# Bias lines as sixteen shifted copies, wide up products in a row, first block and last tile split, TensorE spins

## The chip, the cores and the metric

The kernel runs on one core of a Trainium2 chip. A core has five engines with queues of their own: TensorE (matrix products, PE in the profile, its weight loads PEld), VectorE (DVE), ScalarE (ACT), GpSimd (POOL) and SyncE (SP), which here does nothing but issue DMAs. They meet through semaphores alone. The metric is device time in microseconds of one execution; the median of three runs is given.

## The reference, cut to what matters

Two transformer blocks, in float32, one after the other on the same 256 tokens of 1024 columns. The parts that the change touches:

```python
def first_block(x, ...):                       # layer 0: gated linear attention; layer 1: window attention
    h = x
    h = h + gla_mixer(rmsnorm(h, ln_mix[0]), a_w_in[0], ...)        # a_w_in: 1024 x 3088
    h = h + sq_relu_mlp(rmsnorm(h, ln_mlp[0]), w_up[0], w_down[0])  # up 1024 x 4096, down 4096 x 1024
    kb, vb = shared_kv(rmsnorm(h, kv_norm), w_kv)
    h = h + swa_mixer(rmsnorm(h, ln_mix[1]), kb, vb, ..., rel_table, ...)
    h = h + sq_relu_mlp(rmsnorm(h, ln_mlp[1]), w_up[1], w_down[1])
    return rmsnorm(h, ln_final)

  # swa_mixer:  s = q k^T + rel_table[bucket(i + 128 - j)]     a bias that depends on i - j alone
  # mixer_b:    sc = q k^T + rel_bias[t5_bucket(j - i)]        the same, three dilations, 12 heads

def second_block(x, p, ...):
    x = x + (gate_a * y_a + gate_b * y_b) @ w_out
    x = x + square(relu(rmsnorm_2(x, norm_mlp_g) @ w_ff1)) @ w_ff2
    gate_p = sigmoid(rmsnorm_2(x, norm_ple_g) @ w_ple_gate)         # 1024 x 1024
    x = x + gate_p * (p @ w_ple)
    return rmsnorm_2(x, final_norm_g)
```

## The kernel before, in words

**Products.** Every float32 matrix is held as a high part (rounded, float32r) and a low part (the rest). A product is three float32r products in one PSUM bank: high by high, high by low, low by high (`prod`). Activations are transposed to [column, token], eight groups of 128 columns, high and low (`hT`). 161 weight blocks of up to 128 x 2048 elements pass through three raw buffers and three high and low buffers. For each block SP issues one load (`weights_to`), ScalarE casts it to `whi` (`highs_to`, line 1695), VectorE subtracts to get `wlo` (`lows_to`, line 941, two halves), TensorE multiplies (line 265). SP issues the load of block j when the lows of block j - 3 are done. All loads and stores go through SP's one queue, in program order.

**Order.** Each engine has its own program (`tensor_program`, `vector_program`, `scalar_program`, `pool_program`, `sync_program`), written out by hand with generators (`gemm_a`, `gemm_up`, `gemm_b`) that step through the same blocks on each engine; nothing is reordered at run time. A wait holds its engine's whole queue.

**Start.** SP loads the identity, a gain, x in two halves of 512 columns, then weight block 0. TensorE transposes x in four pairs of 128 columns (`norm_turn`, line 269); ScalarE and VectorE write the high and low part of each pair times the gain; ScalarE casts block 0 and VectorE subtracts; then `gemm_a` multiplies it (two output halves of eight groups). Blocks 0 to 4 are queries, keys and a 16-column gate; 5 to 8 the values; 9 to 12 the output gate.

**Bias.** TensorE makes one line of bias per head with a selection matrix (16 lines of 383, 12 of 511). SP writes the lines to DRAM (`scr1`, `scr2`), then builds in DRAM the full 128-row shifted tables (`toe1` 16 x 128 x 256, `toe2` 12 x 128 x 384) with two DRAM-to-DRAM transfers, between the loads of blocks 6 and 7. Each table is loaded later by one transfer: after block 20, and after block 61.

**Up products.** Three times (both layers and the second block's MLP) `gemm_up` multiplies 1024 x 4096 in 16 blocks, interleaved with the 16 blocks of the down product. Weights stand still, tokens move: for each group of 128 rows one product of 512 columns (the high weights by [high | low] activations, `hT2`, two pieces of 256 columns 2048 elements apart) and one of 256 columns (low weights by high activations), which adds to the second half of the bank. In the first block the eight groups are done in two halves of four, with the transposes of the second half between.

**End.** `gemm_b` multiplies the last gate (`pg`) in four blocks, tokens in two halves c, columns in two halves f. For each of the four tiles: ScalarE's sigmoid, VectorE's product with `pw` and sum into x, ScalarE's square with a sum, GpSimd's mean and power, VectorE's final multiply by row scale and gain, SP's store.

## Time and profile before

| | us |
|---|---|
| median of three runs | 1066.18 (1065.83 to 1066.78) |
| the profiled execution | 1064.24 |
| span of its instructions | 1062.4 |
| TensorE busy | 1012.1 (95%) |
| VectorE, ScalarE, GpSimd busy | 676.2, 489.3, 42.8 |
| chain that ended last: TensorE | 85% |
| 180.99 MB moved by DMA, mean | 170 GB/s |

All profile numbers come from one execution, the one of 1064.24 us; times in its views count from the start of its span. A row of the timeline gives start, duration, engine, line of the code, operation, what is written from what, shape and count; the bracket tells how long the engine was idle before and what ended that. Consecutive instructions of one kind are merged in a row. A product's duration reaches to its modelled end, past the start of the next, so the spacing is read from starts. A chain row gives what TensorE or another engine did, or waited for, on the way to the last instruction.

### The profile page before, as it was taken

What the parts mean: (1) busy time and instruction counts of PE and PEld (TensorE: products, weight loads), DVE (VectorE), ACT (ScalarE), POOL (GpSimd) and SP (SyncE); (2) the same over time, 40 slices, a digit from 0 to 9 for tenths busy, and PEclk for the clock granted to TensorE, in tenths of its full rate; (3) what the DMA queues carried; (4) which work ended last, traced back from release to release, by engine and by line L of the source; (5) the groups of instructions that cost most, each with busy time, mean ns of one, the idle gap of its engine ahead of it and who ended that gap; (6) DMA issues with size and microseconds to landing.
All of it is one profiled execution on the core that took longest, in us unless ns stands there. A gap on an engine that the chain in (4) does not pass through costs nothing.

```text
span 1062.4 us, 12980 instructions
## 1 busy us (share of the span) xinstructions
PE 1012.1 (95%) x5384; PEld 849.5 (80%) x5384; DVE 676.2 (64%) x945; ACT 489.3 (46%) x573; POOL 42.8 (4%) x57
## 2 busy tenths in 40 slices
PE   6989999999999889999999999899999999999996
PEld 5866778888888767888888889877877788888875
DVE  4665766566656885754666656676656675466664
ACT  4353445344445653544444454334563454344452
POOL 1000100000000000000000013300000000000000
PEclk9989999999999999999999999999999999999999
DMA  7772376545564314765455555632335656545451
GB/s 214 249 262 80 119 238 224 173 160 197 199 214 143 120 50 149 250 217 197 159 188 180 201 183 161 196 100 80 99 109 178 195 175 215 188 159 197 180 175 43
DMA packets 115027, 180.99 MB, mean 170 GB/s; under 512 B 4351, under 2 KB 78567, under 8 KB 114968
## 3 DMA queue, kind: packets, MB, share of 16 engines
q1 hardware_dynamic: 114968, 180.16, 50.8%
q8 instruction: 42, 0.69, 0.3%
q14 instruction: 17, 0.14, 0.0%
HBM read 179.05 MB, written 5.55 MB: 174 GB/s over the span
## 4 chain that ended last, share of the span: by engine, by line
PE 85%; DVE 7%; ACT 2%; DMA 2%; POOL 2%; issue 1%; SPq 0%; DVEq 0%; POOLq 0%; ACTq 0%
PE ps L265 82%; PE ps L269 3%; DMA raw<-in_a_w_in 2%; DVE wlo L941 2%; DVE M L949 1%; DVE M L941 1%; POOL st L2186 1%; ACT M L1692 1%; ACT RR L1695 1%; ACT whi L1695 1%; POOL M L2186 0%; DVE M L945 0%; ACT M L1695 0%; DMA x<-in_x 0%; POOL st L2183 0%
## 5 line engine op out<-in xcount | busy, mean ns | idle before, releaser
L265 PE MATMUL ps<-whi,RR 128*128 128x512 f32 (+2 forms) x1568 | 494.6, 390 | 9.7 <-DVE wlo L941 6.0
L1695 ACT ACTIVATE whi<-raw 128x2048 fp32r<-128x2048 f32 (+1 forms) x161 | 302.3, 1881 | 196.6 <-PE ps L265 179.9
L941 DVE TENSOR_TENSOR wlo<-raw,whi 128x1024 fp32r<-128x1024 f32 (+1 forms) x322 | 372.5, 1200 | 29.9 <-ACT whi L1695 29.7
L265 PE MATMUL ps<-RR,whi 128*128 128x512 f32 (+1 forms) x1248 | 362.8, 357 | 10.9 <-DVE RR L949 5.6
L265 PEld LDWEIGHTS ps<-whi,RR 128*128 128x128 f32 x1568 | 293.9, 189 | 74.8 <-issue 9.6
L265 PE MATMUL ps<-wlo,RR 128*128 128x512 f32 (+2 forms) x784 | 303.2, 387 | 0.0
L265 PE MATMUL ps<-RR,wlo 128*128 128x256 f32 (+1 forms) x1008 | 284.5, 282 | 0.0
L265 PEld LDWEIGHTS ps<-RR,whi 128*128 128x128 f32 x1248 | 220.3, 190 | 50.6 <-issue 8.3
L265 PEld LDWEIGHTS ps<-RR,wlo 128*128 128x128 f32 (+1 forms) x1008 | 191.5, 190 | 0.9
L265 PEld LDWEIGHTS ps<-wlo,RR 128*128 128x128 f32 x784 | 148.4, 189 | 27.7
L941 DVE TENSOR_TENSOR M<-M,ps 128x512 f32<-128x512 f32 x56 | 38.5, 687 | 181.7 <-ACT M L1695 173.8
L1695 ACT ACTIVATE M<-ps 128x512 f32<-128x512 f32 (+2 forms) x97 | 57.1, 597 | 173.7 <-PE ps L265 138.5
L265 PE MATMUL ps<-M 128*64 128x128 f32 (+5 forms) x416 | 66.4, 334 | 5.6 <-DVE M L949 2.9
L265 PEld LDWEIGHTS ps<-M 128*64 128x64 f32 (+2 forms) x416 | 46.6, 163 | 22.1 <-issue 13.2
L1695 ACT ACTIVATE RR<-M 128x512 fp32r<-128x512 f32 x48 | 30.4, 633 | 71.1 <-DVE M L949 71.1
L2183 POOL TENSOR_SCALAR st<-st 128x2 f32<-128x2 f32 (+3 forms) x13 | 7.7, 595 | 886.6 <-DVE st L1032 621.3
L269 PE MATMUL ps<-ident,M 128*128 128x128 f32 (+1 forms) x194 | 29.4, 290 | 13.3 <-DVE M L941 4.9
L1695 ACT ACTIVATE RR<-ps,G 128x256 fp32r<-128x256 f32 x64 | 25.1, 480 | 32.9 <-PE ps L269 32.8
L269 PEld LDWEIGHTS ps<-ident,M 128*128 128x128 f32 (+1 forms) x194 | 23.2, 148 | 20.9 <-issue 14.9
L949 DVE SCALAR_TENSOR_TENSOR M<-M 128x512 f32<-128x512 f32 (+1 forms) x49 | 34.4, 703 | 1.6
L949 DVE SCALAR_TENSOR_TENSOR RR<-ps,G,RR 128x256 fp32r<-128x256 f32 x64 | 26.4, 478 | 13.7 <-ACT RR L1695 13.7
L941 DVE TENSOR_TENSOR RR<-M,RR 128x512 fp32r<-128x512 f32 x48 | 32.9, 686 | 0.0
(88 smaller groups left out, 381.7 us busy)
## 6 DMA issues: line engine op xcount, KB each, us to landing
raw<-in_w_up SPq DMA_DIRECT2D x32, 1024.0 KB, 5.4
raw<-in_w_down SPq DMA_DIRECT2D x32, 1024.0 KB, 5.0
raw<-in_w_ff SPq DMA_DIRECT2D x32, 1024.0 KB, 5.3
raw<-in_w_in SPq DMA_DIRECT2D x23, 1024.0 KB, 5.1
raw<-in_a_w_in SPq DMA_DIRECT2D x12, 1024.0 KB, 7.1
raw<-in_a_w_out SPq DMA_DIRECT2D x4, 1024.0 KB, 5.0
raw<-in_b_w_q SPq DMA_DIRECT2D x4, 1024.0 KB, 5.3
raw<-in_b_w_out SPq DMA_DIRECT2D x4, 1024.0 KB, 5.0
```

The lines of the kernel that those rows point to most:

```text
L265: return pe.matmul(out, lhsT, rhs, start=start, stop=stop, skip_group_check=True)
L269: return pe.transpose(out, in_, ident[0:n, 0:n])
L941: return dve.tensor_tensor(out, a, b, op)
L949: return dve.scalar_tensor_tensor(out=out, in0=a, scalar=s, in1=b, op0=op0, op1=op1)
L1692: return act.activation(out, in_, f, **k)
L1695: return act.activation(out, in_, ACT.Copy, **k)
L2183: return pool.tensor_scalar(out, a, s1, s2, op0, op1)
L2186: return pool.tensor_tensor(out, a, b, op)
```

## The change

Four edits.

1. The first weight block is loaded in two halves, each behind one half of x; ScalarE and VectorE treat it in halves between the pairs of transposed columns; TensorE does its first four groups of both output halves before the other four, and the row-scale product one block later. TensorE begins with four products of a matrix of ones by itself, written to a bank that nothing reads, and does five more behind the transpose of the gain. GpSimd writes the ones first.
2. Each bias line is written to DRAM sixteen times, each copy one element further on; the two tables are gone. Each of eight transfers per table fills sixteen rows straight from the copies, one ahead of each of eight weight blocks.
3. `hT` holds high and low of a group next to each other, so that `hT2` is one piece; `gemm_up` does the wide products of a row of groups first, behind the wait for the highs, then the narrow ones behind the wait for the lows.
4. The last quarter of the last gate is done as two tiles of 256 columns. The final gain is multiplied into a second buffer before the row scale is known; ScalarE does the final scale of the first token half, VectorE that of the second; GpSimd adds the sums step by step.

```diff
-        self.hT, self.yT = parts(0), parts(4096)
-        self.hT2 = RR[:, 0:4096].rearrange("p (a k t) -> p k a t", a=2, t=T)
+        self.hT2 = RR[:, 0:4096].rearrange("p (k n) -> p k n", k=8)
+        self.hT, self.yT = (self.hT2[:, :, 0:T], self.hT2[:, :, T:2 * T]), parts(4096)
...
+LAST = [(0, 0, 512), (1, 0, 512), (0, 512, 1024), (1, 512, 768), (1, 768, 1024)]
...
-            for w_ in due(K.at("w_lo", j)):
-                pe.wait_ge(*w_)
...
-                        for w_ in due(ready(k)):
+                        for w_ in due(K.at("w_lo", (0, 0) if j == 0 and k < 4 else j), ready(k)):
                             pe.wait_ge(*w_)
...
-            for w_ in due(K.at("w_lo", j)):
+            for w_ in due(K.at("w_hi", j)):
                 pe.wait_ge(*w_)
...
                     for k in range(k0, k1):
                         for w_ in due(ready(k)):
                             pe.wait_ge(*w_)
-                        mm(b[:, i, :].rearrange("p (a t) -> p a t", a=2), hi[:, k, 128 * i:128 * i + 128],
-                           V.hT2[:, k, :, :], k == 0, False)
+                        mm(b[:, i, :], hi[:, k, 128 * i:128 * i + 128], V.hT2[:, k, :], k == 0, False)
+                    for w_ in due(K.at("w_lo", j)):
+                        pe.wait_ge(*w_)
+                    for k in range(k0, k1):
                         t = mm(b[:, i, T:2 * T], lo[:, k, 128 * i:128 * i + 128], hT[0][:, k, :], False, k == 7)
...
+    def spin(n):
+        for w in due(K.at("ones")):
+            pe.wait_ge(*w)
+        for _ in range(n):
+            mm(K.banks[:, 3, 0:128], V.S["ones"][:, :], V.S["ones"][:, :], True, True)
+    spin(4)
     tile = ("g", 0)
     b = take(tile, misc())
     for w in due(K.dma("id"), K.dma("g0")):
         pe.wait_ge(*w)
     tr(b[:, 0:16], V.M[0:16, 0:128]).then_inc(*K.filled(tile))
+    spin(5)
     norm_rest(0)
...
     def after_qk(f):
-        if f == 0:
+        if f == 256:
             rows_scale(0)
...
-    g = gemm_a(("qk",), W, 0, 1024, hT, h_ready(0), None, after_qk)
+    g = gemm_a(("qk",), W, 0, 1024, hT, h_ready(0), lambda: None, after_qk)
...
-    run_all((gemm_b(("pg",), A["w_ple_gate_2"][0], 0, D, hT, h_ready(6)), 1))
+    ready = h_ready(6)
+    for f in (0, 512):
+        bs = acc_pair()
+        tiles = [(("pg", i), take(("pg", i), misc() if i == 4 else bs[LAST[i][0]])) + LAST[i]
+                 for i in range(5) if LAST[i][1] // 512 * 512 == f]
+        for k0 in (0, 4):
+            j, hi, lo = block(A["w_ple_gate_2"][0][k0 * 128:k0 * 128 + 512, f:f + 512], 4, 512)
+            for tile, b, c, n0, n1 in tiles:
+                for k in range(k0, k0 + 4):
+                    for w in due(K.at("w_lo", j), ready(k)):
+                        pe.wait_ge(*w)
+                    t = prod(b[:, 0:n1 - n0], hT[0][:, k, c * 128:c * 128 + 128], hT[1][:, k, c * 128:c * 128 + 128],
+                             hi[:, k - k0, n0 - f:n1 - f], lo[:, k - k0, n0 - f:n1 - f], k == 0, k == 7)
+                if k0:
+                    t.then_inc(*K.filled(tile))
...
+    def first_low(i):
+        h = slice(1024 * i, 1024 * i + 1024)
+        for w in due(K.at("w_hi", (0, 0) if i == 0 else 0)):
+            dve.wait_ge(*w)
+        tt(V.lo[:, 0, h], V.raw[:, 0, h], V.hi[:, 0, h].bitcast(F32), ALU.subtract).then_inc(
+            *K.up("w_lo", (0, 0) if i == 0 else 0))
+    norm_early(0)
+    first_low(0)
+    norm_turn(0, 2)
+    norm_turn(0, 3)
+    first_low(1)
+    block["lo"] = 1
...
     def ev_qk(f):
-        tile = ("qk", f)
         if f == 0:
             diagonals(0)
+        if f == 256:
             rows_scale(0)
...
+        for f2 in {0: [], 256: [0, 256]}.get(f, [f]):
+            tile = ("qk", f2)
+            for w in due(K.full(tile), *rb(0)):
+                dve.wait_ge(*w)
+            stt(M[:, 2 * f2:2 * f2 + 512], K.bank(tile), 128 ** -0.5 if f2 < 512 else 1.0, RB[:, :], ALU.mult,
+                ALU.mult).then_inc(*K.emptied(tile))
...
-    run_all((gemm_b(1024, 8, ev_pg), 1))
...
+    def add(i):
+        c, n0, n1 = LAST[i]
+        s, xc, n = V.SG[:, c, n0:n1], x[:, c, n0:n1], n0 // 512
+        for w in due(K.empty(("pg", i)), K.empty(("pw", 512 * n, c))):
+            dve.wait_ge(*w)
+        d = step(tt(s, s, V.PW[:, c, n0:n1], ALU.mult))
+        for w in due(d, K.full(("nt", 6, 3)), x_ready(K, 6, c, n)):
+            dve.wait_ge(*w)
+        tt(xc, xc, s, ALU.add).then_inc(*K.up("x_end", i))
...
+    def gain(i):
+        c, n0, n1 = LAST[i]
+        for w in due(K.at("x_end", i), K.dma("fin")):
+            dve.wait_ge(*w)
+        tt(V.SG[:, c, n0:n1], x[:, c, n0:n1], M[:, n0:n1], ALU.mult).then_inc(*K.up("x_gain", i))
...
+    take()
+    take()
+    add(0)
+    add(1)
+    take()
+    gain(0)
+    gain(1)
+    take()
+    for i in (2, 3, 4):
+        add(i)
+    for i in (2, 3, 4):
+        gain(i)
+    for n in range(2):
+        s = V.SG[:, 1, 512 * n:512 * n + 512]
+        for w in due(K.at("rstd", ("end", 1)), K.at("x_gain", 4)):
+            dve.wait_ge(*w)
+        ts(s, s, st[:, 49:50], None, ALU.mult, None).then_inc(*K.up("y_end", (1, n)))
...
+    def first_high(i):
+        h = slice(1024 * i, 1024 * i + 1024)
+        for w in due(K.dma("w_first") if i == 0 else K.dma("w0", 0)):
+            act.wait_ge(*w)
+        copy(V.hi[:, 0, h], V.raw[:, 0, h]).then_inc(*K.up("w_hi", (0, 0) if i == 0 else 0))
+    norm_early(0)
+    first_high(0)
+    norm_turn(0, 2)
+    norm_turn(0, 3)
+    first_high(1)
+    block["hi"] = 1
...
+    def square(i):
+        c, n0, n1 = LAST[i]
+        for w in due(K.at("x_end", i)):
+            act.wait_ge(*w)
+        actf(V.PW[:, c, n0:n1], x[:, c, n0:n1], ACT.Square, scale=1.0 / 32, accum_out=st[:, 40 + i:41 + i]).then_inc(
+            *K.up("end_sq", i))
+    take()
+    take()
+    for i in range(2):
+        sig(i)
+        square(i)
+    take()
+    take()
+    sig(2)
+    sig(3)
+    square(2)
+    sig(4)
+    square(3)
+    square(4)
+    for n in range(2):
+        s = V.SG[:, 0, 512 * n:512 * n + 512]
+        for w in due(K.at("rstd", ("end", 0)), K.at("x_gain", 2)):
+            act.wait_ge(*w)
+        copy(s, s, scale=st[:, 48:49]).then_inc(*K.up("y_first", (0, n)))
...
+        ts(st[:, 52 + c:53 + c], st[:, 40 + c:41 + c], EPS, None, ALU.add, None).then_inc(*K.up("end_sum", c))
+    at = [52, 53]
+    for c, i in ((0, 2), (1, 3), (1, 4)):
+        for w in due(K.at("end_sum", at[c] - 52), K.at("end_sq", i)):
             pool.wait_ge(*w)
-        ts(st[:, 46 + c:47 + c], st[:, 44 + c:45 + c], 1.0 / D, EPS, ALU.mult, ALU.add).then_inc(
...
+        tt(st[:, 52 + i:53 + i], st[:, at[c]:at[c] + 1], st[:, 40 + i:41 + i], ALU.add).then_inc(*K.up("end_sum", i))
+        at[c] = 52 + i
+        if i != 3:
+            for w in due(K.at("end_sum", i)):
+                pool.wait_ge(*w)
+            tt(st[:, 48 + c:49 + c], st[:, at[c]:at[c] + 1], S["half_"][:, 0:1], ALU.pow).then_inc(
+                *K.up("rstd", ("end", c)))
...
     for n in range(2):
         load("x%d" % n, 0, V.x[:, :, n * 512:n * 512 + 512], xd[:, :, n * 512:n * 512 + 512])
+        w = K.blocks[0][0][512 * n:512 * n + 512, :] if K.blocks else A["a_w_in"][0][0:512, 0:256]
+        load("w0" if n else "w_first", 0, V.raw[:, 0, 1024 * n:1024 * n + 1024].rearrange("p (k n) -> p k n", k=4),
+             w.rearrange("(k p) n -> p k n", p=128))
+    state["block"] = 1
...
-    load("scr1", 0, A["scr1"], M[0:16, 14336:14719], K.empty(("br", 0)))
+    line = M[0:16, 14336:14719]
+    load("scr1", 0, bass.AP(tensor=A["scr1"].tensor, offset=0, ap=[[400, 16], [16 * 400 + 1, 16], [1, 383]]),
+         bass.AP(tensor=line.tensor, offset=line.offset, ap=[line.ap[0], [0, 16], [1, 383]]), K.empty(("br", 0)))
     for g in range(3):
-        load("scr2", g, A["scr2"][4 * g:4 * g + 4, :], M[32 * g:32 * g + 4, 14848:15359], K.empty(("br", g + 1)))
-    load("toe1", 0, A["toe1"], bass.AP(tensor=A["scr1"].tensor, offset=127, ap=[[383, 16], [-1, 128], [1, 256]]),
-         K.dma("scr1"))
-    load("toe2", 0, A["toe2"], bass.AP(tensor=A["scr2"].tensor, offset=127, ap=[[511, 12], [-1, 128], [1, 384]]),
-         K.dma("scr2", 2))
+        line = M[32 * g:32 * g + 4, 14848:15359]
+        load("scr2", g, bass.AP(tensor=A["scr2"].tensor, offset=4 * g * 528,
+                                ap=[[528, 4], [12 * 528 + 1, 16], [1, 511]]),
+             bass.AP(tensor=line.tensor, offset=line.offset, ap=[line.ap[0], [0, 16], [1, 511]]),
+             K.empty(("br", g + 1)))
...
-    weights_to(21)
-    load("bias", 0, V.BS, A["toe1"].rearrange("h p c -> p h c"), K.dma("toe1"), K.full(("to", 1, 1)))
-    weights_to(62)
-    load("bias", 1, V.BB, A["toe2"].rearrange("h p c -> p h c"), K.dma("toe2"), K.empty(("pr", 1, 1)))
+    for a in range(8):
+        weights_to(20 + a)
+        load("bias1", a, V.BS[16 * a:16 * a + 16], bass.AP(tensor=A["scr1"].tensor, offset=127 - 16 * a, ap=[
+            [16 * 400, 16], [400, 16], [1, 256]]), K.dma("scr1"), K.full(("to", 1, 1)))
+    weights_to(60)
+    for a in range(8):
+        weights_to(61 + a)
+        load("bias2", a, V.BB[16 * a:16 * a + 16], bass.AP(tensor=A["scr2"].tensor, offset=127 - 16 * a, ap=[
+            [12 * 528, 16], [528, 12], [1, 384]]), K.dma("scr2", 2), K.empty(("pr", 1, 1)))
...
             load("out", 2 * c + n, A["out"][0, c * 128:c * 128 + 128, n * 512:n * 512 + 512],
-                 V.x[:, c, n * 512:n * 512 + 512], K.at("y_end", (c, n)))
+                 V.SG[:, c, n * 512:n * 512 + 512], K.at("y_end" if c else "y_first", (c, n)))
...
-        A["scr1"] = nc.dram_tensor("scr1", (16, 383), F32, kind="Internal").ap()
-        A["scr2"] = nc.dram_tensor("scr2", (12, 511), F32, kind="Internal").ap()
-        A["toe1"] = nc.dram_tensor("toe1", (16, 128, 256), F32, kind="Internal").ap()
-        A["toe2"] = nc.dram_tensor("toe2", (12, 128, 384), F32, kind="Internal").ap()
+        A["scr1"] = nc.dram_tensor("scr1", (16, 16, 400), F32, kind="Internal").ap()
+        A["scr2"] = nc.dram_tensor("scr2", (16, 12, 528), F32, kind="Internal").ap()
```

Where the change moves instructions, the order on two engines follows. Line numbers of the changed kernel are its own. In the rows, `ps` is a PSUM bank, `RR` the activations, `whi` and `wlo` the weights' parts, moving operand first.

TensorE, the program's beginning, before:

```order
L269 MATMUL ps<-ident,M 128x16 [waits d_g0,d_id]
L269 MATMUL ps<-ident,x 128x128 [waits d_x0]
L269 MATMUL ps<-ident,x 128x128 x7
L269 MATMUL ps<-ident,x 128x128 [waits d_x1]
L269 MATMUL ps<-ident,x 128x128 x3
L269 MATMUL ps<-ident,x 128x128 [waits ps4_read]
L269 MATMUL ps<-ident,x 128x128 x3
L265 MATMUL ps<-RR,whi 128x256 [waits w_lo,ps5_read]
```

and now:

```order
L267 MATMUL ps<-ones 128x128 [waits ones]
L267 MATMUL ps<-ones 128x128 x3
L271 MATMUL ps<-ident,M 128x16 [waits d_g0,d_id]
L267 MATMUL ps<-ones 128x128 x5
L271 MATMUL ps<-ident,x 128x128 [waits d_x0]
L271 MATMUL ps<-ident,x 128x128 x7
L271 MATMUL ps<-ident,x 128x128 [waits d_x1]
L271 MATMUL ps<-ident,x 128x128 x3
L271 MATMUL ps<-ident,x 128x128 [waits ps4_read]
L271 MATMUL ps<-ident,x 128x128 x3
L267 MATMUL ps<-RR,whi 128x256 [waits w_lo,ps5_read]
```

The spins stand ahead of the gain's transpose and of x's; further down, the wait for the block's second half stands before the 25th product.

TensorE, the first block of the first up product, before (the rest of the half goes on in the same way):

```order
L265 MATMUL ps<-RR,whi 128x512 [waits ps4_read,w_lo]
L265 MATMUL ps<-RR,wlo 128x256
L265 MATMUL ps<-RR,whi 128x512
L265 MATMUL ps<-RR,wlo 128x256
L265 MATMUL ps<-RR,whi 128x512 [waits ps5_read]
L265 MATMUL ps<-RR,wlo 128x256
```

and now, with the beginning of the second half:

```order
L267 MATMUL ps<-RR,whi 128x512 [waits ps4_read,w_hi]
L267 MATMUL ps<-RR,whi 128x512
L267 MATMUL ps<-RR,whi 128x512 [waits ps5_read]
L267 MATMUL ps<-RR,whi 128x512
L267 MATMUL ps<-RR,wlo 128x256 [waits w_lo]
L267 MATMUL ps<-RR,wlo 128x256 x3
L267 MATMUL ps<-RR,whi 128x512 x4
L267 MATMUL ps<-RR,wlo 128x256 x4
L271 MATMUL ps<-ident,x 128x128 [waits ps2_read]
L271 MATMUL ps<-ident,x 128x128 [waits ps3_read]
L271 MATMUL ps<-ident,x 128x128 x6
L267 MATMUL ps<-RR,whi 128x512 [waits ps4_read]
```

Four wide products stand in a row, then four narrow ones, where they alternated.

SP, from the bias lines on (`scr` the lines in DRAM, `toe` the tables, `raw` weight blocks), before:

```order
L2293 DMA scr<-M 16x383 [waits ps6_read]
L2293 DMA scr<-M 4x511 [waits ps7_read]
L2293 DMA scr<-M 4x511 [waits ps4_read]
L2293 DMA scr<-M 4x511 [waits ps5_read]
L2293 DMA toe<-scr 2048x1x256 [waits d_scr1]
L2293 DMA toe<-scr 1536x1x384 [waits d_scr2]
L2303 DMA raw<-in_a_w_in 128x4x512 [waits w_lo] x2
```

and now:

```order
L2389 DMA scr<-M 16x16x383 [waits ps6_read]
L2389 DMA scr<-M 4x16x511 [waits ps7_read]
L2389 DMA scr<-M 4x16x511 [waits ps4_read]
L2389 DMA scr<-M 4x16x511 [waits ps5_read]
L2399 DMA raw<-in_a_w_in 128x4x512 [waits w_lo] x2
```

The two transfers to `toe` are gone from between the lines and the loads of blocks 7 and 8. Sixteen-row pieces (`M<-scr 16x16x256`) stand further down, one ahead of the fourth block of the first up product and of each of the seven behind it, where one load of a table stood behind the fourth.

## Rows read from the trace of the kernel before

**Rows 1.** The page, busy time, share of the span and count by engine.
```profile
PE 1012.1 (95%) x5384; PEld 849.5 (80%) x5384; DVE 676.2 (64%) x945; ACT 489.3 (46%) x573; POOL 42.8 (4%) x57
```

**Rows 2.** TensorE's busy time (count), granted clock, DMA share, GB/s in seven stretches.
```profile
14.38:20.21 5.83, 5.83 (x27) 1.00 0.73 205
23.44:28.83 5.39, 5.39 (x47) 1.00 0.90 297
61.23:65.66 4.43, 0.20 (x1) 0.88 0.72 265
65.67:71.41 5.74, 5.74 (x14) 0.50 0.58 194
152.30:324.80 172.50, 172.50 (x870) 1.00 0.57 193
869.81:878.66 8.85, 8.85 (x41) 1.00 0.73 262
879.11:883.69 4.58, 4.58 (x27) 1.00 0.87 305
```

**Rows 3.** Timeline of the start: start, us, engine, line, operation, count.
```profile
5.50 3.67 PE L269 MATMUL ps<-ident,x 128*128 128x128 f32 x16 [2.17 <-DMA x<-in_x]
6.65 3.40 ACT L1695 ACTIVATE RR<-ps,G 128x256 fp32r<-128x256 f32 x8 [1.74 <-PE ps L269]
7.61 3.35 DVE L949 SCALAR_TENSOR_TENSOR RR<-ps,G,RR 128x256 fp32r<-128x256 f32 x8 [4.06 <-ACT RR L1695]
9.94 1.91 ACT L1695 ACTIVATE whi<-raw 128x2048 fp32r<-128x2048 f32 x1
...
11.88 2.36 DVE L941 TENSOR_TENSOR wlo<-raw,whi 128x1024 fp32r<-128x1024 f32 x2 [0.92 <-ACT whi L1695]
...
15.30 2.35 DVE L941 TENSOR_TENSOR wlo<-raw,whi 128x1024 fp32r<-128x1024 f32 x2
```

**Rows 4.** DMA issues, us to landing, stretches 2.2:2.5 and 2.7:3.0.
```profile
x<-in_x SPq DMA_DIRECT2D x1, 512.0 KB, 4.7
...
raw<-in_a_w_in SPq DMA_DIRECT2D x1, 1024.0 KB, 7.2
```

**Rows 5.** Chain that ended last, 30 to 75 us: start, us, what.
```profile
40.08 21.20 DMA raw<-in_a_w_in
...
65.67 8.42 PE ps L265 x24
```

**Rows 6.** Timeline of VectorE and of ScalarE, 28 to 110 us.
```profile
58.02 1.22 DVE L941 TENSOR_TENSOR M<-M 128x1024 f32<-128x1024 f32 x1
...
64.53 2.95 ACT L1692 ACTIVATE M<-M 128x1024 f32<-128x1024 f32 x3
```

**Rows 7.** DMA issues of the whole run: count, KB, us to landing.
```profile
M<-toe SPq DMA_DIRECT2D x1, 2048.0 KB, 12.4
...
scr<-M SPq DMA_DIRECT2D x1, 23.9 KB, 4.3
```

**Rows 8.** Timeline of VectorE and of TensorE, 149.5 to 153.8 us.
```profile
151.30 1.66 DVE L949 SCALAR_TENSOR_TENSOR RR<-ps,G,RR 128x256 fp32r<-128x256 f32 x4 [1.16 <-ACT RR L1695]
...
152.23 0.50 PE L265 MATMUL ps<-RR,whi 128*128 128x512 f32 x1 [1.40 <-DVE RR L949]
```

**Rows 9.** Timeline of the end.
```profile
1053.38 0.39 PE L265 MATMUL ps<-whi,RR 128*128 128x512 f32 x1
...
1053.89 0.67 ACT L1692 ACTIVATE M<-ps,st 128x512 f32<-128x512 f32 x1
...
1058.34 1.41 DVE L949 SCALAR_TENSOR_TENSOR x<-x,st,M 128x512 f32<-128x512 f32 x2 [1.00 <-POOL st L2186]
...
1059.12 0.99 SPq L2293 DMA_DIRECT2D out<-x  x2
```

**Rows 10.** Groups by shape: count, busy us, mean ns, idle before.
```profile
L1692 ACT ACTIVATE M<-ps,cc 128x256 f32<-128x256 f32 x16 | 7.4, 470 | 16.2 <-DVE cc L945 16.2
...
L941 DVE TENSOR_TENSOR RR<-ps,RR 128x256 fp32r<-128x256 f32 x18 | 7.6, 422 | 6.1 <-ACT RR L1695 5.8
```

58 lines of the change are left out of this document (14 added, 44 removed).

## The prediction

> **What bounds the kernel now.** I read the page first: TensorE is busy 95% of the span [rows 1], so a microsecond counts only where TensorE waits, where its products are spaced wider than they need be, or behind its last product. The view of busy time by stretch comes next, since it counts products and names the granted clock [rows 2]. In all four places that the change touches, TensorE loses something: it starts its first weight product at 14.38 and runs 27 of them in 5.83 us (216 ns each, against 120 ns later for the same shape: the 1.2 GHz level by the spacing, although the column still reads 1.00); it stands still before 65.67 and then works at a granted clock of 0.50; in the up products a pair takes more than its two halves do elsewhere; and 9.0 us pass between the start of the last product and the end. The timeline of the start, the chain of waits, and the tail give the steps [rows 3, 5, 9].
>
> **First block split, and spins.** Today the first product waits for all eight transposed columns and the whole weight block: ScalarE writes eight gains (0.43 us each from 6.65) and casts the block in 1.91, VectorE subtracts for 2.36, end 14.24 [rows 3]. The loads keep one queue: the second half of x lands 4.7 us after its issue at about 2.1, thus at 6.8, and the first 1 MB block at about 2.6 + 7.2 = 9.8, 3.0 us for a megabyte [rows 4]. Afterwards half a block (1.5 us) stands ahead of the second half of x, so x is complete at 8.3 and the block, as before, at 9.8. ScalarE: four gains to 8.35, half a cast to 9.4, four gains to 11.1, half a cast to 12.2. VectorE is one step behind: half the lows at 10.65, four gains to 12.35, the other half to 13.6. TensorE stands in order behind the transposes of the late half of x (8.3 to 10.0), which are done before 10.65, so they cost nothing. It starts at 10.8; 24 products at 120 ns end at 13.7, 24 more at 16.6. Block 1 then waits: ScalarE squares x (1.1) behind its cast at 12.2, casts block 1 (1.9), VectorE subtracts (2.35): 17.65, the very time of today [rows 3], because this chain does not get shorter. Block 1 begins at 17.8 instead of 22.73 (20.21 + 21 x 0.120). The row-scale product only changes its place. A later evacuation (the low products' 16-row tile, now behind two evacuations and a low) takes back some 0.25 us on a PSUM bank. Gain 4.9 - 0.3 = **4.6 us**. It rests on the clock: nine spins and sixteen transposes fill most of 1.0 to 10 us, and the rows show the level rising twice after some 5.8 us of unbroken work (14.38 to 20.21, 65.67 to 71.41 [rows 2]); the 3.67 us of transposes alone did not raise it [rows 3]. If it stays low, the first 24 products take 5.2 us and the sum is 3.4 us: the lower end. The later half of the small loads leaves SP only 0.6 us earlier; the blocks that it feeds are wanted several microseconds after they land, so nothing is lost there.
>
> **Bias lines.** Two DRAM-to-DRAM writes of 2.0 and 2.25 MB leave the queue; behind them block 7 took 21.2 us to land [rows 5], and TensorE, whose last product of block 6 starts just before 61.23, has 0.20 us of work until block 7 begins at 65.67 [rows 2]. They are replaced by four writes of 0.78 MB together. At the rate of the 2 MB load (12.4 us [rows 7]) that is 4.7 us; if each of the four took the 4.3 us of today's 24 KB write [rows 7], 17 us, and block 7 would land near 58. (It cannot go by bytes from that row, as 1 MB lands in 7.2 us at worst in [rows 4].) I take 4.7, since rows of 1 to 2 KB are moved in both; either way the load itself costs at most 0.7 us. What is late next is VectorE: its subtraction for the gates ends at 58.02 + 1.22 = 59.24 [rows 6], the lows of block 7 follow, 2.36, so TensorE starts at 61.65. Twenty-four products at 227 ns end at 67.1. Next in TensorE's order are transposes of the decayed keys: VectorE multiplies queries and keys (twice 1.2, as at 58.02; ScalarE's three exponentials take 2.95 [rows 6] and no longer queue behind the block-7 cast), subtracts block 8 (2.36) and multiplies the decayed keys (1.22), 67.5. Today block 7 ended near 74.0 because its products ran at a granted 0.50 until 71.41 [rows 2, 5]. So 74.0 - 67.6 = **6.4 us**, with 4.4 (only the standstill goes) and 7.0 (no wait at 67.1) as ends.
> The rest of the part moves loads: two of 2.0 and 2.25 MB become sixteen of 256 to 288 KB, one ahead of each weight block of the two first up-and-down products. By today's load a piece takes 12.4 / 8 = 1.55 us. A weight block has 172.5 us / 30.5 = 5.65 us, and the engines are busy 0.57 of it [rows 2], which leaves 2.4 us: hidden. The first piece of the second set waits for the last evacuation of the attention output with one more weight block now behind it; that block is the fourth to be used, three block times of 5.65 us later. Cost 0.
>
> **Up product.** All 768 pairs of a 512-column and a 256-column product are reordered, wide ones in a row, and the wide operand becomes one piece of memory instead of two. In the mixed stream 26 products start in 4.58 us, 352 ns a pair. A stream of 512-column products alone has 39 starts in 8.85 us, 226.9 ns; one of 256-column products 45 starts in 5.39, 119.8 [rows 2] (one or two products run into each stretch and are in its count). Together 346.7, 5.6 ns less: 768 x 5.6 = 4.3 us. Against it: in the first chunk of each of the three up products TensorE resumes behind VectorE's four lows of 1.66 us [rows 8]. Today it does wide, narrow, wide, narrow there while the second pair of lows is made; in a row, the third wide one is reached after 0.55 us and waits some 0.3 us, 0.8 us in three chunks. Net **3.5 us**, ends 4.3 gained and 0.8 lost. The wait on the highs instead of the lows frees nothing, since lows are long done in these stages.
> A rule speaks against this term. The Trainium skill, "TensorE: Matmul & The Clock Gate", section "Back-to-back issue gap", gives the spacing of products as columns over 2.4 GHz plus 2.5 ns, so that a pair takes the same time in any order. The unmixed streams here carry 13 ns each over their columns, not 2.5; whether the 5.6 ns on top belong to the order no run here shows.
>
> **Last tile split.** Today, from the start of the last product (1053.38): sigmoid 1053.89, two VectorE steps, square, three GpSimd steps, two final multiplies from 1058.34 to 1059.75, that is 6.37 us, then issue and landing to 1062.4 [rows 9]. Afterwards the last tile has 256 columns: product to sigmoid 0.40, sigmoid 0.47, two VectorE steps of 0.42 [rows 10], square and its sum 0.5, add and power 0.9 to 1.2, two multiplies by a scalar 0.9, hops 0.2: 4.2 to 4.5. The gain multiplies fit in between the square and the power. That is 2.0 less; the two halves cost 48 x 0.120 - 24 x 0.227 = 0.31 more on TensorE. Net **1.5 us**, ends 0.9 and 2.0.
>
> **Sum.** 4.6 + 6.4 + 3.5 + 1.5 = 16.0. The profiled run took 1064.24 us, 1.94 below the median of 1066.18: 1064.24 - 16.0 = 1048.2, on the median 1050.2. The stages between are bound by TensorE and move forward whole.
>
> **Rivals.** (1) Spacing is set by columns alone: the 352 ns remain, only the new 0.8 us wait is left, 16.0 - 4.3 = 11.7 gained, 1054.5. For it: VectorE and ScalarE cannot cause it, and both widths carry an equal fixed part. Against it: a pair is longer than its parts, and both things that differ are removed. The section cited above would have it so. 0.18. (2) The spins do not do what they are for and the level rises only during the first block: 14.8 gained, 1051.4. For it: the transposes did not raise it. 0.17. (3) Slower: a bias piece, written to 16 rows, moves at a fraction of today's rate and holds up the weight block behind it in the same queue, sixteen times. Beyond 2.4 us a piece the queue falls behind, with some 6 us in hand per product (loads run two blocks ahead); at 5 us a piece 2 x (8 x 2.6 - 6) = 29.6 lost, 1079.8; it outweighs the gains from 4.2 us a piece. Against it: 1.55 us by [rows 7]. 0.05. The Trainium skill, "SBUF — State Buffer", section "Door 1", has 16 partitions reach 4 of 16 ports, 104 GB/s against 328 for 128; an estimate from it is 2.5 us a piece, just at the room of 2.4, which would still leave the sum as it is; no run here shows it.
>
> **How the numbers follow.** Forecast 1050.2, chance 0.57, its own range 1047.9 (all upper ends) to 1053; (1) 0.18, (2) 0.17, (3) 0.05, the rest for cases between. Range 1046.5 to 1056.5, which takes in (1) and (2), and (1) with (2) at 1055.7. A measurement can tell about 0.2% (2.1 us): faster 0.93, same 0.02, slower 0.05.
>
> **What would show it.** Right: first weight product near 10.8 at 120 ns; no granted 0.50 around 65; block 7 landing in 10 us or less; 347 ns a pair; the last issue about 5 us behind the last product's start. Wrong: casts of weights that wait for DMA in the first two up products; 216 ns in the first block; 352 ns a pair with a wait of 0.3 us in each first chunk.

## The result, and the profile after

The changed kernel takes 1054.26 us (median of four runs, 1053.28 to 1056.38), the kernel before, on the same chip, 1066.01. The ratio is 0.9898, with an interval of 0.9872 to 0.9925: 11.8 us less where 16.0 were forecast. The time lies inside the range, 4.1 us above the forecast and above the forecast's own range of 1047.9 to 1053. That it lies 0.2 us from rival (1)'s 1054.5 is chance: the mechanism of that rival is refuted below (experiments 3 and 4). The profiled execution took 1055.0 us, its span is 1053.2.

The page of the changed kernel, busy time by engine (the answer to [rows 1]):

```profile
PE 1014.0 (96%) x5426; PEld 853.6 (81%) x5426; DVE 677.0 (64%) x950; ACT 491.5 (47%) x579; POOL 42.7 (4%) x58
```

The page counts 42 product records more on TensorE (each of the nine spins is two records, and the split last quarter adds 24), and the span is 9.2 us shorter. Where those come from is read from the starts of the same instructions in both traces. Each number says by how many microseconds the instruction starts earlier than in the kernel before:

| TensorE's place (start before) | forecast | changed | changed, again | no spins | copies in DRAM |
|---|---|---|---|---|---|
| block 1 (23.02; the forecast counts from 22.73) | 4.9 | 5.4 | 5.1 | 5.2 | 5.2 |
| transposes of the decayed keys (73.92) | 11.0 | 9.2 | 9.0 | 8.7 | 11.0 |
| first up product, second half (152.23) | 11.0 | 7.7 | 9.0 | 8.7 | 9.5 |
| second up product (424.35) | 12.2 | 7.1 | 9.7 | 8.4 | 8.7 |
| third up product (848.58) | 13.3 | 7.9 | 10.4 | 8.8 | 9.4 |
| last product (1053.38) | 14.2 | 8.0 | 10.5 | 8.9 | 9.5 |
| end of the span (1062.4) | 16.0 | 9.2 | 11.8 | 10.2 | 10.8 |

("Changed, again" is the same kernel, profiled a second time; the last two columns are experiments below. In the first row 0.3 us of each measured number are the row-scale products, which only change their place: counted from 22.73 it is 5.1, 4.8, 4.9 and 4.9.) The first block gains what was forecast. Then 1.8 us are missing at the decayed keys; the up products add less than 1.2 us each; the tail adds 1.2 to 1.3 where 1.8 were expected; and in the attention stages of the first trace 2.8 us are lost that the second keeps (1.5 between the decayed keys and the first up product, 1.3 before the second).

The start on VectorE and TensorE, timeline of the changed kernel (start, duration, what):

```profile
9.14 1.23 DVE L970 TENSOR_TENSOR wlo<-raw,whi 128x1024 fp32r<-128x1024 f32 x1
...
15.18 2.36 DVE L970 TENSOR_TENSOR wlo<-raw,whi 128x1024 fp32r<-128x1024 f32 x2 [0.76 <-ACT whi L1755]
```

```profile
8.80 1.09 PE L271 MATMUL ps<-ident,x 128*128 128x128 f32 x8 [1.77 <-DMA x<-in_x]
10.51 0.77 PE L267 MATMUL ps<-RR,whi 128*128 128x256 f32 x2 [0.62 <-DVE wlo L970]
...
17.59 0.50 PE L267 MATMUL ps<-RR,whi 128*128 128x256 f32 x2
```

The lows of the block's first half are done at 10.37 and the product starts at 10.51; block 1 starts at 17.59 behind its lows (15.18 + 2.36). Forecast were 10.65, 10.8 and 17.8. One of the prediction's signs of being wrong appears all the same: the first dozen products start 213 ns apart, at a granted 0.50 from 9.92 to 13.34, and TensorE's own 48 products end only at 17.59, together with those lows.

The same kernel's chain that ended last, 28 to 66 us, against [rows 5]:

```profile
32.52 3.71 SPq L2389
...
36.28 16.72 DMA raw<-in_a_w_in
...
64.70 0.63 PE ps L271 x4
```

The 21.20 us of block 7's load are now 16.72, not under 10. SP itself is held (3.71 us to issue one of the copies). But this row is not yet the key to the 1.8 us. VectorE in the same trace (the multiplication for the gates, the lows of block 7, those of block 8):

```profile
54.90 1.23 DVE L970 TENSOR_TENSOR M<-M 128x1024 f32<-128x1024 f32 x1
56.05 2.35 DVE L970 TENSOR_TENSOR wlo<-raw,whi 128x1024 fp32r<-128x1024 f32 x2
...
61.05 2.36 DVE L970 TENSOR_TENSOR wlo<-raw,whi 128x1024 fp32r<-128x1024 f32 x2 [0.20 <-ACT whi L1755]
```

The lows of block 7 do not wait. VectorE comes to the multiplication at 54.90, where it comes at 53.59 without spins and at 53.61 with the copies in DRAM, in two traces that have no stretch at 0.50 around 30. Between 31 and 37 us TensorE's place falls from 0.3 to 1.3 us behind the trace without spins. So some 1.3 of the 1.8 us go to the stretch from 30.40 to 33.82 (below), and some 0.5 to waits behind block 7; in the second trace (54.90 becomes 55.15) it is 1.5 of 2.0. Where that stretch is missing, the late landing alone costs 2.3 us (experiment 6).

TensorE's granted clock in stretches of the changed kernel (busy time and counts by engine, then granted clock, DMA share, GB/s), and below it, when the same kernel was profiled again, its own stretch at 31.52 and the stages that stood at 85.02 and 351.26:

```profile
9.92:13.34 3.42, 2.83 (x13) 2.86 (x14) 3.40 (x7) 3.24 (x8) 0.00 (x0) 0.50 0.88 237
30.40:33.82 3.42, 3.42 (x14) 2.94 (x14) 3.30 (x4) 2.69 (x2) 0.00 (x0) 0.50 1.03 364
85.02:88.43 3.41, 3.41 (x8) 1.08 (x6) 0.00 (x0) 0.00 (x0) 0.00 (x0) 0.50 0.00 0
351.26:354.67 3.41, 2.88 (x14) 2.92 (x15) 3.27 (x11) 1.85 (x7) 0.20 (x1) 0.50 0.29 117
```

```profile
31.52:34.94 3.42, 3.42 (x19) 3.42 (x18) 2.72 (x3) 1.91 (x1) 0.00 (x0) 0.50 0.99 326
85.22:88.63 3.41, 3.41 (x14) 1.81 (x13) 0.59 (x3) 1.26 (x2) 0.00 (x0) 1.00 0.02 5
350.00:353.40 3.40, 2.88 (x25) 2.91 (x26) 3.26 (x11) 1.85 (x7) 0.20 (x1) 1.00 0.32 131
```

The stretch at 0.50 around 65 [rows 2] is gone, as forecast; others came. Of the four shown, two (85.0 and 351.3) are missing in the second trace of the same kernel; the other two come again, 1.1 us later. Its stage at 350 does 25 products where the first did 14, and its stage at 85 does fourteen where the first did eight.

### The profile page after: what moved, and what is told of

It reads as the page before. It is cut to its first block, busy times and chain, and to the rows that moved or that the text cites. A ratio compares the mean times of both kernels' runs of the same rounds, so it can differ in the third digit from the quotient of the medians.

```text
span 1053.2 us, 13094 instructions
## 1 busy us (share of the span) xinstructions
PE 1014.0 (96%) x5426; PEld 853.6 (81%) x5426; DVE 677.0 (64%) x950; ACT 491.5 (47%) x579; POOL 42.7 (4%) x58
## 3 DMA queue, kind: packets, MB, share of 16 engines
HBM read 174.60 MB, written 1.83 MB: 168 GB/s over the span
## 4 chain that ended last, share of the span: by engine, by line
PE 82%; DVE 8%; ACT 3%; DMA 2%; POOL 2%; issue 1%; SPq 0%; POOLq 0%; DVEq 0%; ACTq 0%
PE ps L267 79%; PE ps L271 3%; DVE wlo L970 2%; DMA raw<-in_a_w_in 2%; DVE M L978 1%; DVE M L970 1%; ACT M L1752 1%; POOL st L2279 1%; ACT whi L1755 1%; DVE M L974 1%; DVE RR L978 1%; SPq L2389 0%; ACT RR L1755 0%; POOL M L2279 0%; ACT M L1755 0%
## 5 line engine op out<-in xcount | busy, mean ns | idle before, releaser
L1755 ACT ACTIVATE whi<-raw 128x2048 fp32r<-128x2048 f32 (+2 forms) x162 | 302.6, 1871 | 192.6 <-PE ps L267 155.5
L267 PE MATMUL ps<-RR,whi 128*128 128x512 f32 (+1 forms) x1248 | 285.9, 354 | 6.5 <-DVE RR L978 5.6
L267 PEld LDWEIGHTS ps<-RR,whi 128*128 128x128 f32 x1248 | 215.2, 191 | 37.8 <-DVE RR L978 8.5
L267 PE MATMUL ps<-RR,wlo 128*128 128x256 f32 (+1 forms) x1008 | 177.1, 284 | 0.0
L267 PEld LDWEIGHTS ps<-RR,wlo 128*128 128x128 f32 (+1 forms) x1008 | 152.2, 191 | 8.2
L1755 ACT ACTIVATE RR<-M 128x512 fp32r<-128x512 f32 x48 | 30.4, 633 | 71.1 <-DVE M L978 71.1
L2276 POOL TENSOR_SCALAR st<-st 128x2 f32<-128x2 f32 (+2 forms) x11 | 6.5, 594 | 882.8 <-DVE st L1061 618.8
```

The source lines that it names most:

```text
L267: return pe.matmul(out, lhsT, rhs, start=start, stop=stop, skip_group_check=True)
L1755: return act.activation(out, in_, ACT.Copy, **k)
L2276: return pool.tensor_scalar(out, a, s1, s2, op0, op1)
```

## Experiments

The kernels ran in three groups (1 to 4, 5 to 8, 9 to 12), each on one chip beside the kernel before, whose medians there are 1063.13, 1064.03 and 1065.17.

**1. No spins.**

```diff
-    spin(4)
-    spin(5)
```

> The changed kernel without its nine products of ones at the start. Theory (clock): in the changed kernel the spins brought the 2.4 GHz level at 6.5 us, but a stretch at a granted 0.50 from 9.92 to 13.34 took it back, so only some 13 of the first 24 weight products were spared. Without spins the level rises during the first block: the first 24 products at 213 to 216 ns, block 1 starting 0 to 1.2 us later than the 17.59 of the changed kernel, and the whole 0 to 1.5 us slower than it (1053 to 1056). Rival (the spins carry most of the start's gain): block 1 starts at 19 or later and the whole is over 2 us slower. Second question: if the 0.50 stretches at 30.4 and 85.0 follow from the early lift, they are gone here, and the whole is 1 to 3 us faster.

Measured: 1053.64 (1053.21 to 1055.25), ratio 0.991, 0.9895 to 0.9925: the changed kernel's time. TensorE, timeline without spins:

```profile
17.78 0.50 PE L267 MATMUL ps<-RR,whi 128*128 128x256 f32 x2 [0.76 <-DVE wlo L968]
```

The spacing falls from 213 to some 118 ns at 11.7 by itself; block 1 starts 0.2 us later than with spins, after a wait for VectorE's lows. The spins are worth nothing that the times show. But that VectorE sets block 1 is not general: over all traces 1 to 17 of the first 24 products are slow with the spins and 5 to 19 without them, and with many slow ones TensorE comes last. In the second trace of the changed kernel 17 are slow, and block 1 starts at 17.95, 0.65 us behind its lows. In this trace the stretches at 30 and 85 are at 1.00, but experiments 5 and 6 below, also without spins, have one of them or both again.

**2. More spins,** which fill TensorE's standstills at 7.0 and 9.9.

```diff
-    norm_rest(0)
+    norm_early(0)
+    spin(6)
+    norm_turn(0, 2)
+    norm_turn(0, 3)
+    spin(2)
```

> The changed kernel with six more products of ones between the two halves of the transposes (7.03 to 8.80, where TensorE stands still for 1.77 us) and two before the first weight product. Theory (the 0.50 stretch at 9.92 follows that standstill): no granted 0.50 before 13.3, the first 24 products at 120 ns (10.5 to 13.4). Block 1 still starts at 17.5 because VectorE's second lows set it, so this by itself gives at most 0.3 us; if the stretch at 30.4 goes with it, another 1.5 to 2.0 us. Rival (the stretches come whatever TensorE did just before): 0.50 again near 9.9 and 30.4, 213 ns in the first half, time as the changed kernel within 0.5 us.

Measured: 1054.5 (1053.81 to 1055.14). Stretches of this kernel:

```profile
10.30:13.20 2.90, 2.90 (x25) 2.90 (x24) 2.76 (x5) 2.81 (x6) 0.00 (x0) 1.00 0.89 224
29.90:36.70 6.80, 6.80 (x27) 5.13 (x25) 4.10 (x5) 2.12 (x2) 0.00 (x0) 0.50 0.76 222
```

The first half of the block runs at 2.4 GHz, as the theory had it, and TensorE then waits 1.16 us for the lows of block 1. The stretch at 30 did not go along; it is longer. So that half of the expectation fell. Nor is the filled standstill shown to be the reason: two kernels of other experiments with the changed kernel's own start (3 and 8) had no 0.50 before 29 either.

**3. and 4. The order alone, and the layout alone.** First the wide operand in two pieces again, order kept (`hT` as before, and the wide product reads the two pieces):

```diff
-        self.hT2 = RR[:, 0:4096].rearrange("p (k n) -> p k n", k=8)
+        self.hT2 = RR[:, 0:4096].rearrange("p (a k t) -> p k a t", a=2, t=T)
...
```

> The changed kernel with the old layout of the activations, so that the wide operand is two pieces of 256 columns again; only the order (wide products in a row) is kept. Theory (the order makes the spacing): 64 products of the up product take 11.15 us as in the changed kernel (348 ns a pair). Rival (the two pieces make it): 11.29 us, 353 ns a pair.

Then one piece, with wide and narrow products alternating (the wait for the lows comes first again):

```diff
...
                         mm(b[:, i, :], hi[:, k, 128 * i:128 * i + 128], V.hT2[:, k, :], k == 0, False)
-                    for w_ in due(K.at("w_lo", j)):
-                        pe.wait_ge(*w_)
-                    for k in range(k0, k1):
                         t = mm(b[:, i, T:2 * T], lo[:, k, 128 * i:128 * i + 128], hT[0][:, k, :], False, k == 7)
```

> The changed kernel with wide and narrow products alternating as before; only the layout in one piece is kept. Theory (the order makes the spacing): 64 products take 11.29 us as before the change (353 ns a pair), the first chunks lose their new waits (second half of the first chunk back to the old pace), so the whole is 2 to 2.5 us slower than the changed kernel. Rival (the layout makes it): 11.15 us, and the whole is 1 to 2 us faster than the changed kernel.

Measured: 64 products of the third up product, from their first start to the start of the next product, in the changed kernel, order alone, layout alone, and in the kernel before (one to two products of the neighbours are in the counts):

```profile
871.64:882.78 11.14, 11.14 (x65) 9.82 (x64) 4.25 (x5) 4.96 (x4) 0.00 (x0) 1.00 0.35 122
```

```profile
871.14:882.28 11.14, 11.14 (x65) 9.82 (x64) 4.25 (x5) 4.96 (x4) 0.00 (x0) 1.00 0.35 126
```

```profile
872.09:883.38 11.29, 11.29 (x66) 9.82 (x64) 4.25 (x5) 4.96 (x4) 0.00 (x0) 1.00 0.35 124
```

```profile
879.11:890.40 11.29, 11.29 (x65) 9.79 (x64) 4.25 (x5) 4.96 (x4) 0.00 (x0) 1.00 0.36 124
```

The order does it, the layout nothing: 348.3 ns a pair against 352.8. In starts, the order alone gains 1.0, 0.7 and 0.7 us in the three up products, as the changed kernel does; the layout alone gains 0.3, then loses 0.5 and 0.3. Times: 1056.12 and 1056.68, two runs each, too few to order them. One part of the expectation was wrong: with the layout alone the first chunk of the second and third up product takes 19.97 us, as in the changed kernel, where 19.61 (before) was expected. There the alternating stream itself was slower, at 353 ns a pair, than in the kernel before, at 347 (last section).

**5. Copies not shifted against each other** (without spins; `scr1` in the same way). The kernel leaves out the shift, so the bias that it adds is another.

```diff
-                                ap=[[528, 4], [12 * 528 + 1, 16], [1, 511]]),
+                                ap=[[528, 4], [12 * 528, 16], [1, 511]]),
```

> Without spins, and with the sixteen copies of a bias line not shifted against each other (the same bytes and rows, but every copy starts on the same boundary; the bias that is added is therefore another). In the changed kernel without spins block 7 lands at 53.55, 16 us behind its issue, and in 36 to 50 us the queue moves only 23 to 50 GB/s. Theory (a copy is read from four rows of the on-chip memory, and four rows give little): nothing changes, block 7 lands at 52 to 54. Rival (writes that start 4 bytes apart are slow): block 7 lands before 45, and the transposes of the decayed keys start near 63.2 instead of 65.25.

Measured: block 7 lands at 53.79, 17.67 us behind its issue; 1056.11 us. Alignment is not it. What the queue moves from 28 to 57 us in the changed kernel, in forty slices (busy share of 16 DMA engines in tenths, GB/s):

```profile
DMA  9999999993223222258999478997425632277999
GB/s 379 387 322 305 347 401 398 363 206 57 23 23 48 25 28 23 25 59 147 271 330 328 102 138 229 319 328 243 116 71 170 211 122 102 106 129 207 380 408 379
```

From 34.5 to 40 us two to three tenths of the engines are busy, at 23 to 57 GB/s. The three copies of 128 KB that come from four rows are moving, and block 7 waits behind them. The other one, 383 KB from sixteen rows, landed 6.0 us after its issue. The Trainium skill, "DMA: Bandwidth & Descriptors", section "Why a DMA increments its semaphore by 16 and not by 1", has a transfer spread over the largest number of engines, up to 16, that divides the slowest dimension of both sides. By that rule four rows occupy four of 16 engines, and the busy share here agrees. So do the packets in the trace: the 192 packets of 2044 bytes of these copies run from 34.3 to 50.1 us, some four at a time. But the number of engines is only part of the price: four of 16 would leave, as an estimate, a quarter of the 380 GB/s that weight blocks reach at the beginning of this stretch, some 95. Each of these packets takes some 0.30 us, where the 2048 bytes of a weight block's packet take 0.08; why, no run here shows.

**6. Copies made inside DRAM** (without spins). Block 7's load now also stands ahead of the copies in the queue, so the run does not separate the other way of copying from the other order.

```diff
+    load("line1", 0, A["line1"], M[0:16, 14336:14719], K.empty(("br", 0)))
+    for g in range(3):
+        load("line2", g, A["line2"][4 * g:4 * g + 4, :], M[32 * g:32 * g + 4, 14848:15359], K.empty(("br", g + 1)))
+    weights_to(8)
     load("scr1", 0, bass.AP(tensor=A["scr1"].tensor, offset=0, ap=[[400, 16], [16 * 400 + 1, 16], [1, 383]]),
+         bass.AP(tensor=A["line1"].tensor, offset=0, ap=[[383, 16], [0, 16], [1, 383]]), K.dma("line1"))
...
```

> Without spins; the bias lines are written to DRAM once, and behind the load of block 7 two DRAM-to-DRAM transfers make the sixteen shifted copies from them (0.78 MB). Theory (the late landing of block 7 holds VectorE for 0.71 + 0.28 + 1.07 us before the transposes of the decayed keys at 65.25): block 7 lands at 35 to 41, VectorE has no wait there, the transposes start at 63.0 to 63.4, and the whole takes 2.0 us less than without spins alone (about 1051.6). Rival (something else is late there, or the two transfers hold up block 8): the transposes stay at 65 and the time at 1053.6.

VectorE without spins alone, and then with the copies in DRAM (the bracket is the wait before):

```profile
55.53 2.36 DVE L968 TENSOR_TENSOR wlo<-raw,whi 128x1024 fp32r<-128x1024 f32 x2 [0.71 <-ACT whi L1753]
58.16 2.36 DVE L968 TENSOR_TENSOR M<-M 128x1024 f32<-128x1024 f32 x2 [0.28 <-POOL ebl L2314]
61.60 2.36 DVE L968 TENSOR_TENSOR wlo<-raw,whi 128x1024 fp32r<-128x1024 f32 x2 [1.07 <-ACT whi L1753]
```

```profile
54.75 2.36 DVE L968 TENSOR_TENSOR wlo<-raw,whi 128x1024 fp32r<-128x1024 f32 x2
57.04 2.35 DVE L968 TENSOR_TENSOR M<-M 128x1024 f32<-128x1024 f32 x2
59.31 2.35 DVE L968 TENSOR_TENSOR wlo<-raw,whi 128x1024 fp32r<-128x1024 f32 x2
```

The three waits are gone, and the transposes start at 62.94 instead of 65.24: 11.0 us ahead of the kernel before, the forecast's own 4.6 + 6.4. Neither of the two traces has a stretch at 0.50 before this place. The median did not follow: 1053.81 (1052.77 to 1055.86), ratio 0.9907 (0.9881 to 0.9934), though that interval is wide enough to hold 2 us. In this trace a 0.50 stretch from 83.7 to 87.1 takes back 1.5 us, and one at 349.9 as much again. And where a stretch at 30 delays VectorE as in the changed kernel's two traces, there are only some 0.5 us to be had here.

**7. The first row of groups alternating again** in the first block of each up product.

```diff
+                    turned = [[k] for k in range(k0, k1)] if len(halves) == 2 and i == 0 else [range(k0, k1)]
+                    for ks in turned:
...
```

> The changed kernel, but in the first block of each up product the first row of groups alternates wide and narrow products again (in both halves). Theory (a row of four wide products meets transposed columns that are not yet written: 338, 448 and 338 ns instead of 227): four pairs after the standstill take 1.59 us instead of 1.83, so 0.25 us in each of the three up products, 0.2 more in the first half of layer 1; 0.7 to 0.9 us less in all than the changed kernel. Rival (the first chunk is slower for another reason): the 112 products of the first chunk still take 19.97 to 20.0 us.

TensorE where it resumes in the third up product: the changed kernel, then this one.

```profile
840.73 1.52 PE L267 MATMUL ps<-RR,whi 128*128 128x512 f32 x4 [1.40 <-DVE RR L978]
842.09 0.64 PE L267 MATMUL ps<-RR,wlo 128*128 128x256 f32 x4
842.56 0.86 PE L267 MATMUL ps<-RR,whi 128*128 128x512 f32 x3
```

```profile
838.70 0.50 PE L267 MATMUL ps<-RR,whi 128*128 128x512 f32 x1 [1.40 <-DVE RR L980]
...
840.17 0.28 PE L267 MATMUL ps<-RR,wlo 128*128 128x256 f32 x1
840.29 1.11 PE L267 MATMUL ps<-RR,whi 128*128 128x512 f32 x4
```

The first four pairs take 1.83 us in the changed kernel and 1.59 here; the first chunk 19.75 instead of 20.00, in each of the three. So 0.25 us each is the price of the row of wide products at this place. Time: 1053.64, two runs.

**8. Bias pieces twice.**

```diff
+        if a < 7:
+            load("spare1", a, V.BS[16 * a + 16:16 * a + 32], bass.AP(tensor=A["scr1"].tensor, offset=127 - 16 * a, ap=[
+                [16 * 400, 16], [400, 16], [1, 256]]), K.dma("scr1"), K.full(("to", 1, 1)))
```

(and the same for the second set; the next piece waits until the spare one has landed)

> The changed kernel with fourteen of the sixteen bias pieces loaded a second time (to rows that the next piece fills), so that each weight block waits behind twice the bytes. Theory (a piece into sixteen rows costs 2.5 to 3.8 us of the queue, read from the landings of blocks 24 to 27 of the changed kernel, and not 1.55): a block and two pieces take some 9 us where a block's turn is 5.6, so the queue falls 3.4 us behind in each of seven turns, less some 8 to 12 us in hand: 10 to 15 us lost in each of the two up products, 1074 to 1084. Rival (a piece costs 1.55 us): 6.1 against 5.6, all of it covered, time as the changed kernel.

Measured: 1073.15 (1069.5 to 1073.69), ratio 1.0075 (1.0049 to 1.01). TensorE's two longest new waits, and the clock behind the second:

```profile
442.84 0.79 PE L267 MATMUL ps<-whi,RR 128*128 128x512 f32 x1 [3.13 <-DVE wlo L970]
...
472.41 0.80 PE L267 MATMUL ps<-whi,RR 128*128 128x512 f32 x1 [4.94 <-DVE wlo L970]
```

```profile
469.80:476.60 6.80, 4.19 (x10) 3.36 (x11) 3.19 (x5) 3.02 (x3) 0.00 (x0) 0.50 1.00 254
```

The first up product loses only 3.4 us by its starts (2.9 of them waits of 1.75 and 1.10), not 10 to 15; the second 13.4, of which 8.1 are these waits and most of the rest the clock behind them. Another 2.1 go to a stretch at 0.50 from 698 to 709. A block with two pieces takes 7.2 to 8.0 us of the queue (it lands at 443.76, 451.06, 459.07, 466.22 and 474.12), one with a single piece, at the same place in the changed kernel, 5.3 to 6.1. The second piece thus adds some 1.8 us. Without pieces, blocks behind this place land some 3 us apart (480.49 and 483.48), which leaves 2.1 to 2.5 us for each of two pieces. The queue from 430 to 470 us with doubled pieces, in slices of one microsecond:

```profile
GB/s 246 406 332 182 114 134 140 131 389 401 151 204 103 144 105 126 318 349 243 228 111 147 107 121 278 349 327 197 106 147 120 125 255 410 264 214 109 129 121 130
```

While pieces move it carries 103 to 151 GB/s, while blocks move up to 410. At 120 GB/s a piece of 288 KB takes 2.5 us. The prediction has an estimate of 2.5 us from the Trainium skill, "SBUF — State Buffer", section "Door 1"; the trace agrees with it better than with my 1.55. In the changed kernel single pieces use up the room without passing it: ScalarE's casts wait for loads (total us, times, longest), which the same view of the kernel before does not list for these weights; TensorE's waits there are the same as before.

```profile
ACT whi L1755 <- DMA raw<-in_w_down: 8.9, 3, 4.8
ACT whi L1755 <- DMA raw<-in_w_up: 7.1, 4, 3.3
```

In other kernels with the same single pieces the room is passed: TensorE waits for the lows of such a block for 0.29 us in experiment 2, 0.28 in 5, 0.34 in 7 and 0.58 in 11. In experiment 7:

```profile
462.50 0.50 PE L267 MATMUL ps<-whi,RR 128*128 128x512 f32 x1 [0.34 <-DVE wlo L972]
```

The chain behind this wait leads over the lows and the cast to a load of `w_down` that took 13.8 us. Over the products that the kernel before does from 447 to 507 us, the lead over it falls by 0.7 us there; in the second trace of the changed kernel it rises by 0.1.

**9. The changed kernel again,** unchanged.

> The changed kernel itself once more, beside the three others on one chip. The ratio to the kernel before stays at 0.990 (0.987 to 0.9925), 1053 to 1056. Theory (where the clock falls to 0.50 is not set by the program alone): of the stretches that the changed kernel showed at 9.9, 30.4, 85.0, 351 and 375 at least one is missing or elsewhere, and the runs' mean granted clocks spread from 0.988 to 0.997 as before. Rival (they follow from the program): the same five stretches within 0.5 us.

Measured: 1054.13 (1052.42 to 1056.21), ratio 0.990 (0.9885 to 0.9915). Its profile is of the fastest run, with 0.50 up to 400 us only at 11.0, 31.5 and 372.9. Of the 2.6 us between the two profiles of one kernel, the stages at 85 (1.5) and 350 to 380 (1.3) hold all, less 0.2 by which the first was ahead. So the program alone does not fix where the clock falls, though the stretches at 10, 31 and 373 to 375 come in both.

**10. Four changes together:** no spins, copies in DRAM, first row alternating (as in 1, 6 and 7), a piece ahead of every second block (shown).

```diff
-        weights_to(20 + a)
+        weights_to(20 + 2 * a)
...
-        weights_to(61 + a)
+        weights_to(61 + 2 * a)
```

> The changed kernel without spins, with each bias line written once and copied sixteen times inside DRAM, with wide and narrow products alternating in the first row of groups of each up product, and with a bias piece ahead of every second weight block instead of every one. By the single runs: 0.75 us from the alternation, 2 us from block 7 landing early where no stretch at a granted 0.50 takes it back, and no cast that waits for DMA in the two up products, which costs TensorE nothing either way. Expected 1.5 to 2.7 us under the changed kernel in the same call (ratio to before 0.9875). If low-clock stretches take back what waits give, it is no more than 0.8 us faster.

Measured: 1055.11 (1051.35 to 1055.9), ratio 0.9895 (0.9877 to 0.9913). That is the changed kernel, not 1.5 to 2.7 us less; 1051.35 is the shortest run of all kernels, but four of six lie above 1054.9. No cast of the MLPs waits for a load any more, and the first chunks take 19.75. What takes it back, in the profiled run (1055.9):

```profile
29.90:36.70 6.80, 6.80 (x27) 5.19 (x24) 4.04 (x5) 2.05 (x2) 0.00 (x0) 0.50 0.59 184
681.90:692.10 10.20, 10.20 (x29) 7.23 (x26) 6.75 (x11) 2.83 (x3) 0.00 (x0) 0.50 0.20 53
```

The transposes of the decayed keys start at 65.8, 2.9 us behind those of experiment 6, with no wait on VectorE behind block 7: the first stretch alone. The second stretch costs 2.1 us (8.7 ahead of the kernel before, then 6.6). Whether more waiting for loads would have meant fewer such stretches, or this is chance, six runs don't tell.

**11. The bias part alone,** put into the kernel before (the edits of the diff above for `scr`, `bias` and `toe`, nothing else).

> The kernel before with the bias part alone (sixteen copies, sixteen pieces, no tables in DRAM). Theory (the terms of the sum overlap, because the copies let block 7 land at 53 to 57 whatever the start gains): block 7 lands at 54 to 57, not 61.29; VectorE's chain through 59.24 sets the rest, the transposes of the decayed keys start at 67.4 to 67.9 instead of 73.92, no granted 0.50 at 64.6; 6.0 to 6.5 us faster than before by itself, so the first block's split added only some 2.9 of the 9.2 us that the changed kernel had there. Rival (bias gives less alone): 5 us or less, start at 69 or later.

Measured: 1060.57 (1057.85 to 1062.04), ratio 0.9954 (0.9938 to 0.997), which is 3.2 to 6.6 us less; the medians differ by 4.6, on the rival's side of 5. In the profiled run (1057.85, the fastest of five) it is 6.2 us at the decayed keys and 6.4 at the end. Its chain:

```profile
59.53 2.38 DVE wlo L941 x2
...
61.95 5.74 PE ps L265 x24
...
67.72 0.63 PE ps L269 x4
```

Block 7 lands at 55.10, VectorE's lows end at 61.9, and the transposes start at 67.72: the forecast for this part, step by step (61.65, 67.1, 67.5), with nothing of the first block's split in it. So the path is the theory's, and the time is left open. Of the changed kernel's 9.2 us in the first trace the split therefore adds 3.0, and in experiment 6 4.8.

**12. The last quarter in one tile.**

```diff
-LAST = [(0, 0, 512), (1, 0, 512), (0, 512, 1024), (1, 512, 768), (1, 768, 1024)]
+LAST = [(0, 0, 512), (1, 0, 512), (0, 512, 1024), (1, 512, 1024)]
```

> The changed kernel with the last quarter of the last gate as one tile of 512 columns again; the early gain, the scale by two engines and the stepwise sum stay. Theory (halving the last tile shortens what stands behind the last product by four steps of some 0.25 us and a shorter product, and costs 0.31 to 0.57 us on TensorE): the last product starts 0.3 to 0.6 us earlier than with the split, the end comes 8.6 to 9.0 us behind it instead of 7.8, and the whole is 0.4 to 0.8 us slower. Rival (the other edits made the shorter tail): 8.0 us or less behind the last product, and no loss.

Measured: 1054.22, two runs. The last product of this kernel, and below it of the changed one, each with VectorE's last multiplies:

```profile
1043.06 0.39 PE L267 MATMUL ps<-whi,RR 128*128 128x512 f32 x1
...
1047.62 0.88 DVE L974 TENSOR_SCALAR M<-M,st 128x512 f32<-128x512 f32 x2 [0.73 <-POOL st L2277]
```

```profile
1045.41 0.28 PE L267 MATMUL ps<-whi,RR 128*128 128x256 f32 x1
...
1048.85 0.88 DVE L974 TENSOR_SCALAR M<-M,st 128x512 f32<-128x512 f32 x2 [0.46 <-POOL st L2279]
```

Behind the last product stand 8.7 us here (span 1051.7), 7.8 in the changed kernel, 9.0 before. The split costs 0.4 us on TensorE (25.2 us from the cast of block 158 to the last product, 24.8 here) and saves 0.9 behind it: 0.5 net, near the lower end of what was expected. The two medians can't show that.

## Why the prediction was right, and where not

**First block, 4.6.** Right as far as block 1 (17.59 against 17.8) and on VectorE's chain (lows done at 17.54). Wrong on the clock: the spins raised it, but it fell again, and a dozen products or more ran at 213 ns, with block 1 at 17.59 and 17.95 in the two traces. Rival (2) priced that at 1.2 us for 24 slow products; no trace of a kernel with the split had all 24, and a dozen or so fit in ahead of the lows, so that it cost 0 to 0.65. That block 1 came out right so closely in the first trace is partly luck. A PSUM wait behind the bias lines was 0.30 (forecast 0.25).

**Bias lines, 6.4.** As a part alone right in its path, step by step (6.2 and 6.4 in the trace of experiment 11; 4.6 by the medians). The step that failed is the one on the copies: 4.7 us by the rate of the 2 MB load of a table, "either way the load itself costs at most 0.7 us". The copies from four rows are moving until 50.1, and block 7 lands at 53.00; I had the end "17 us, near 58", but set it against VectorE's unshifted time. With the split, VectorE comes 4.8 us earlier (54.75 in experiment 6 against 59.53 in 11) and block 7 only 2.1 (53.00 against 55.10). Where the clock lets VectorE come so early, 2.3 us of the sum of 11.0 are lost, and experiment 6 gives them back; in the changed kernel's own traces a stretch at 0.50 holds VectorE back by 1.3 and 1.5 us, and the landing costs only some 0.5 on top. The two terms were added as if independent.

**Pieces, 0.** In both traces of the changed kernel the cost was right, the price not: about 1.8 to 2.5 us instead of 1.55, so the room of 2.4 is just used up, and in four of the other kernels passed by 0.3 to 0.6 us of waits. Rival (3) stood closer than 0.05 says: twice the piece costs 19 us.

**Up product, 3.5.** Rival (1) is refuted; the spacing depends on the order. 4.5 ns a pair came of the 5.6; a further 0.04 us at each change to the down product makes up for it (a period of four blocks is 22.055 instead of 22.235 us). The mis-sized term is the new wait: in the second and third up product the first chunk takes 0.38 us more than before (20.00 against 19.61) where a gain of 0.25 was due. Of the 0.63 between, 0.25 is the row of wide products (forecast 0.3); the rest is that the kernel before had run these two chunks at 347 ns a pair already. In the second trace the three products add 1.0, 0.7 and 0.7: 2.4 together. The Trainium skill, "TensorE: Matmul & The Clock Gate", section "Back-to-back issue gap", gives the formula that the prediction took from it as the gap of an isolated product, and says that in a stream weight load and product set the spacing together; of the order it says nothing. So it was no rule against this term, and the runs decide it: 348.3 against 352.8 ns.

**Tail, 1.5.** 0.7 to 0.8 net. (The prediction's own 2.0 less 0.31 is 1.7; it took 1.5.) The chain to the last multiply was right (it ends at 1049.73, 4.3 behind the last product), and so was the last issue (4.65). The landing was not: four stores follow each other on SP within 2 us, the last is issued 0.33 after its data is ready and lands 2.64 after its issue, where the last store of before took 2.19 from issue to landing.

**What was not in the sum:** the clock after the first block. Of 16.0 forecast, the second trace misses 2.0 at the decayed keys (1.5 by the stretch at 31.5, some 0.5 by the copies), 1.1 in the up products, 0.3 between the first two of these and 0.8 in the tail; that leaves its 11.8. The first trace has 2.6 less, all in stretches at a granted 0.50. The trace of the kernel before has such stretches too [rows 2], so each of these differences compares two single executions with stretches of their own.

## What to carry to other kernels

Add the gains of two parts only after asking which absolute time lies between them: a landing that does not move as far as the work that waits for it caps their sum. Then ask what else could hold up the same place: here a stretch at a low clock and a late load each delay it, and removing one leaves the other. Price a transfer by a row with the same number of on-chip rows on its narrow side, not by its bytes. Where two profiles of one kernel differ by 2.6 us through the clock, judge a part by the starts of its own instructions, and the kernel by medians of several runs.

## What was not expected of the hardware

- **Where the clock falls is not fixed by the program alone.** Up to 400 us, the same kernel fell to 0.50 at 9.9, 30.4, 85.0, 351.3 and 375.2 in one run, and at 11.0, 31.5 and 372.9 in another. Before 30.4 TensorE did the bias lines' products after a wait of 0.30, before 85.0 it stood still for 1.06; without spins (experiment 1) the same waits had no fall at 30 or 85, but experiments 5, 6 and 10, also without spins, had one of them or both again.
- **Copies from four rows are slow,** 23 to 57 GB/s, and hold what is queued behind them; with the same bytes copied between DRAM tensors, behind block 7's load, block 7 landed at 39.35 instead of 53.55 and block 8 at 47.55 instead of 56.23. Pieces into sixteen rows move at 103 to 151 GB/s, weight blocks at up to 410.
- **One alternating stream has two paces.** In the kernel before, the first chunk of the third up product ran at 347 ns a pair (below, starts 850.16, 850.51, 850.86), all later ones at 353; in experiment 11, with the same TensorE program, the first chunks of the first two up products ran at the faster pace and the third at the slower. Its cause stays open.

```profile
850.16 0.39 PE L265 MATMUL ps<-RR,whi 128*128 128x512 f32 x1
...
850.51 0.39 PE L265 MATMUL ps<-RR,whi 128*128 128x512 f32 x1
...
850.86 0.39 PE L265 MATMUL ps<-RR,whi 128*128 128x512 f32 x1
```
